# Down projections of two feed-forward layers in seven-product block form

## What is computed

```
f = (silu(h @ w_gate) * (h @ w_up)) @ w_down        # first block: x = x + gate_f * rmsnorm(f) * g
return (silu(h @ w_gate) * (h @ w_up)) @ w_down      # second block: h = h + swiglu(...), then rmsnorm_2(h)
```

## Time and profile before

| what | us |
|---|---|
| runs | 1657.09, 1657.15, 1659.39; median 1657.15 |
| span of the profiled execution | 1655.0, so about 2.15 lie outside the span |
| PE busy | 1628.8 (98%) |
| DVE busy | 1050.5 (63%) |
| ACT busy | 766.2 (46%) |
| POOL busy | 732.0 (44%) |
| first down projection, PE | 467.6 to 591.4 |
| second down projection, PE | 1520.9 to 1645.8 |

### The profile page before, as it was taken

How to read it: one execution, slowest core, us unless ns; L and a number is a source line. 1 busy time by engine, 2 the same in 40 slices (tenths; PEclk the granted TensorE clock), 3 DMA queues, 4 the chain that set the end, 5 groups by cost and what they waited for, 6 DMA issues and landing times.

```text
span 1655.0 us, 24390 instructions
## 1 busy us (share of the span) xinstructions
PE 1628.8 (98%) x9460; PEld 1399.6 (85%) x9460; DVE 1050.5 (63%) x1396; ACT 766.2 (46%) x1029; POOL 732.0 (44%) x540
## 2 busy tenths in 40 slices
PE   7999999999999999999999999999999999999997
PEld 4787899999988898888888887887888789999887
DVE  6777758999920065578778788775113699996102
ACT  4756455455543355334444546544223445544322
POOL 3342343333376635443543434445444443335663
PEclk9999999999999999999999999999999999999999
DMA  8565223333243333233332323223233323332432
GB/s 290 208 225 179 91 89 115 115 105 115 86 150 105 108 115 121 98 102 102 102 105 87 119 85 115 90 90 97 95 112 119 126 83 117 112 111 82 150 97 68
DMA packets 65127, 193.49 MB, mean 117 GB/s; under 512 B 5984, under 2 KB 8288, under 8 KB 64000
## 3 DMA queue, kind: packets, MB, share of 16 engines
q1 hardware_dynamic: 65024, 192.06, 35.3%
HBM read 183.59 MB, written 8.45 MB: 116 GB/s over the span
## 4 chain that ended last, share of the span: by engine, by line
PE 90%; DVE 7%; ACT 1%; issue 1%; DMA 1%; SPq 0%; DVEq 0%
PE PR L778 18%; PE PR L779 18%; PE PR L784 18%; PE PR L1182 4%; PE PR L1189 4%; PE PR L1184 4%; PE AX L1182 3%; PE AX L1189 3%; PE AX L1184 3%; PE PR L795 1%; PE PR L796 1%; PE PR L794 1%; PE AX L1003 1%; PE AX L1330 1%; PE AX L1334 1%
## 5 line engine op out<-in xcount | busy, mean ns | idle before, releaser
L703 POOL TENSOR_TENSOR wlo<-raw,whi 128x512 fp32r<-128x512 f32 (+1 forms) x456 | 605.8, 1354 | 631.3 <-ACT whi L1461 631.3
L1461 ACT ACTIVATE whi<-raw 128x1024 fp32r<-128x1024 f32 x216 | 225.9, 1052 | 150.0 <-PE PR L784 127.2
L778 PE MATMUL PR<-h3h,whi 128*128 128x512 f32 x608 | 245.5, 404 | 0.0
L779 PE MATMUL PR<-h3l,whi 128*128 128x512 f32 x608 | 240.4, 395 | 0.0
L722 POOL TENSOR_TENSOR wlo<-raw,whi 128x512 fp32r<-128x512 f32 x72 | 119.1, 1675 | 239.8 <-ACT whi L1719 239.8
L784 PE MATMUL PR<-h3h,wlo 128*128 128x512 f32 x608 | 154.2, 395 | 0.0
L1182 PE MATMUL PR<-ch,whi 128*128 128x256 f32 x560 | 136.0, 282 | 2.0 <-DVE gate L2509 1.2
L784 PEld LDWEIGHTS PR<-h3h,wlo 128*128 128x128 f32 x608 | 114.2, 188 | 27.6
L778 PEld LDWEIGHTS PR<-h3h,whi 128*128 128x128 f32 x608 | 114.3, 188 | 26.6 <-issue 1.2
L779 PEld LDWEIGHTS PR<-h3l,whi 128*128 128x128 f32 x608 | 114.4, 188 | 26.4 <-issue 1.0
L1184 PE MATMUL PR<-cl,whi 128*128 128x256 f32 x560 | 135.7, 281 | 0.0
(11 more groups left out here) (480 smaller groups left out, 3619.2 us busy)
## 6 DMA issues: line engine op xcount, KB each, us to landing
raw<-w SPq DMA_DIRECT2D x224, 512.0 KB, 3.4
cond<-wcond SPq DMA_DIRECT2D x48, 512.0 KB, 4.2
raw<-w SPq DMA_DIRECT2D x32, 384.0 KB, 3.2
raw<-w SPq DMA_DIRECT2D x32, 320.0 KB, 2.9
x_keep<-x SPq DMA_DIRECT2D x3, 2048.0 KB, 7.3
x<-x_keep SPq DMA_DIRECT2D x2, 2048.0 KB, 8.4
abc_a<-acum_rows SPq DMA_DIRECT2D x8, 512.0 KB, 3.9
abc_b<-acum_rows SPq DMA_DIRECT2D x8, 512.0 KB, 4.5
```

The lines of the kernel that those rows point to most:

```text
L703: ins = pool.tensor_tensor(wlo[:, j, a:a + n], raw[:, j, a:a + n], whi[:, j, a:a + n], ALU.subtract)
L778: pe.matmul(bank, whi[:, j, w], part_of(oh, k0 + k), start=first and i == 0, stop=False)
L779: pe.matmul(bank, whi[:, j, w], part_of(ol, k0 + k), start=False, stop=False)
L1461: act.activation(whi[:, j, :], raw[:, j, :], ACT.Copy).then_inc(hi_ready, 1)
```

## The change

Input tiles 4 to 19 of both down projections go into the seven-product form: input tiles in pairs (eight pairs, `PAIRS`), output tiles in pairs (four groups g, `DN_GROUPS`) and tokens in halves. The six other input tiles (`ALONE`: 0, 1, 2, 3, 20, 21) stay ordinary, as two units O1 and O2 per group. The three old row ranges and their loops are gone. Per group PE runs seven products of 24 matmuls with 256 columns and O1 and O2 with 36 matmuls of 256 columns each: 240 matmuls with 256 columns, against 132 with 512 columns. The order in a group is `DN_A`, and in the last group `DN_B`, where O1 and O2 are split by token half around S4.

What comes with it:

- Token operands: each product needs a combination of the four (input parity, token half) parts. The difference t3 and the term t1 of each pair are made by POOL inside the quads (`third`: two instructions, `third_low`: one, with 256 elements each) with one ACT instruction (`third_high`). At the start of each down projection DVE makes t2, t1l, t4a, t2l, t4b and t4l and POOL the low part of the fourth block (`last_low`), each one instruction with 2048 elements per partition, and ACT the highs b22, t1, t2 and t4, also with 2048.
- Weights: per group DVE makes four sums with 1024 elements (`dn_sum`) and the lows of units 0, 1, 3, 5 and 7 in the order of the group (`dn_low`), POOL those of units 2, 4, 6 and 8.
- Results: DVE combines the seven results (`dn_take`: p3, p4, two, g, then c12, c21, c22; in the second block also x12, x21, x22 and c11), ACT copies two of them (`take_one`, `take_c11`), squares the blocks (`dn_square`), and DVE adds the squares (`dn_acc`).
- `quad_ff_low` and `quad_ff_high` are one instruction with 512 elements per quad instead of two.
- Loads: one block A is eight weight tiles out of every second one, in runs of 512 bytes; O1 and O2 are two DMAs each.
- In the first block x is restored into `xo_a` and `xo_b` and the down result lies in `mixd`; in the second x is restored (2 MB) early in group 0, ahead of the loads of A21(1), A22(1) and O2.
- `mix_sum(3)` waits for the last accumulation of squares, which DVE makes inside `half_h(2)`, behind its second low part; two of the takes (c12, c22) stand inside `half_x(2)`.

```diff
-DOWN_K = [(0, 6), (6, 6), (12, 5), (17, 5)]
+PAIRS = 8
+ALONE = (0, 1, 2, 3, 20, 21)
+DN_A = ("A11", "S3", "A12", "S1", "S2", "S4", "O1", "A22", "O2")
+DN_B = ("A11", "S3", "A12", "S2", "A22", "S1", "S4", "O1", "O2")
...
+            def load_dn(f, g, name):
...
+                half = w22[m].rearrange("p (k two c) -> p k two c", two=2, c=P)[:, 2:10, int(name[2] == "2"), :]
+                sp.dma_start(raw[:, j, :].rearrange("p (k c) -> p k c", c=P), half).then_inc(raw_in[j], 16)
...
+            def third(s):
...
+                pool.tensor_tensor(t3[f][:, k, :], b2[:, 1, k, :], b2[:, 0, k, :], ALU.subtract).then_inc(third_ready, 1)
...
+                pool.tensor_tensor(b2[:, 0, k, :], b2[:, 0, k, :], gate_1[:, 0:T // 2], ALU.subtract).then_inc(third_ready, 1)
...
+            def last_low(f):
...
+                pool.wait_ge(*tp_at(f, "t2"))
+                pool.tensor_tensor(b2l[:, 1, :, :], b2[:, 1, :, :], b22h[:, :, :], ALU.subtract).then_inc(tl_ready, 1)
...
+            def dn_operand(f, name):
+
+                return {"A11": (b1h[:, 0, :, :], b1l[:, 0, :, :]), "A12": (b1h[:, 1, :, :], b1l[:, 1, :, :]),
+                        "S3": (t3h[f], t3l[f]), "S1": (t1h, b2l[:, 0, :, :]), "S4": (b22h, b2l[:, 1, :, :]),
+                        "S2": (t2h, t2l), "A22": (t4h, t4l)}[name]
...
-            x_sum(2)
-            mix_sum(3, V_DN1 + N_DN)
+            x_sum(2)
+            mix_sum(3, *dacc_at(0, 15), ssum_d)
...
+            def dn_first(f):
+
+                end = QUADS * f + QUADS - 1
+                token_part(f, "t2")
+                dn_ahead(f, 0, 0)
+                token_part(f, "t1l")
+                dn_sum(f, 0, "S4")
+                token_part(f, "t4a")
+                token_part(f, "t2l")
+                dn_ahead(f, 0, 1)
+                dn_ahead(f, 0, 2)
+                join(end, 6)
+                quad_ffs(end)
+                quad_ff_low(end)
+                dve.memset(ssum_d[:, :], 0.0).then_inc(dacc, 1)
+                dn_take(f, 0, "p3")
+                dn_take(f, 0, "p4")
+                token_part(f, "t4b")
+                dn_ahead(f, 0, 3)
+                dn_ahead(f, 0, 4)
+                dn_take(f, 0, "two")
+                dn_take(f, 0, "g")
+                token_part(f, "t4l")
...
+            def late_sum(k):
+
+                if k in (0, 1):
+                    dn_acc(0, DN_GROUPS - 1, "c12" if k == 0 else "c22")
```

More of the change, by code:

```diff
@@ L266, in phase_f @@
-            a("above_hth", [P, 1088])
-            ff.update({n: a(f"fq{n}", [P, 4, T], F32R) for n in (8, 9)})
-            fh_end = a("fh_end", [P, 2, T], F32R)
[L269 to L272, removed]
+                b1h = a("b1h", [P, 2, PAIRS, N], F32R, s)
+                b1l = a("b1l", [P, 2, PAIRS, N], F32R, s)
@@ new lines, in phase_f @@
+            alone.append(a("alone_b", [P, 2, 4, T], F32R))
+            fh_end = a("fh_end", [P, 2, T], F32R)
+            with ExitStack() as s:
+                up_2, turn = a("up_2", [P, T], F32, s), a("turn", [P, 8], F32, s)
+            wdt2, twice = a("wdt2", [P, 64 * KT + 64], F32R), a("twice", [P, 32])
+            return (b1h, b1l, xo_a, xo_b, hth, b2, b2l, t3, t3l, t3h, alone, t2, t4, t2l, t2h, t4l, t4h, sqx, t1h, b22h,
+                    one, two, g22, ssum_d, sq_d, wdtr, fh_end, up_2, turn, wdt2, twice)
@@ L274, in phase_first_quad @@
+        (b1h, b1l, xo_a, xo_b, hth, b2, b2l, t3, t3l, t3h, alone, t2, t4, t2l, t2h, t4l, t4h, sqx, t1h, b22h,
+         one, two, g22, ssum_d, sq_d, wdtr, fh_end, up_2, turn, wdt2, twice) = region(phase_f)
         def phase_first_quad(a):
@@ new lines, in dn_slot, with dn_loaded, dn_sum_at @@
+        def dn_slot(g, name):
+            return ({"A21": 2, "A22": 3, "A11": 0, "A12": 1, "O1": 2, "O2": 3}[name] + 2 * g) % RING
+        def dn_loaded(f, g, name):
+            upto = sum(DN_LOADS[n] for h in range(g + 1) for n in DN_BLOCKS if dn_slot(h, n) == dn_slot(g, name) and (
+                h < g or DN_BLOCKS.index(n) <= DN_BLOCKS.index(name)))
+            return raw_in[dn_slot(g, name)], 16 * (loads(U_DN[f]) // RING + upto)
+        def dn_sum_at(f, g, name):
+            return sum_ready, SUMS_FF * f + 4 * QUADS + 4 * g + ("S1", "S3", "S2", "S4").index(name) + 1
@@ L734, in _ @@
             units(U_GU1 + 4, U_ST1)
-            for s, i in POOL_LOWS:
-                quad_low(s, i)
-            units(U_DN1, U_SC)
+            blocks(0)
             for u in range(U_SC, U_SC + 4):
@@ L742, in _ @@
             units(U_SC + 4, U_ST2)
-            for s, i in POOL_LOWS:
-                quad_low(QUADS + s, i)
-            units(U_DN2, U_END - 4)
-            for u in range(U_END - 4, U_END):
-                lo(0, u)
+            blocks(1)
         @block.tensor
@@ L806, in with_low, with mix_sum @@
                 return pe.matmul(PR[:, j, c], whi[:, j, k * P:(k + 1) * P], part_of(ol, k, c), start=False, stop=k == KT - 1)
[L808 to L811 removed]
+            def mix_sum(q, ready, v, src):
+                pe.wait_ge(ready, v)
+                pe.matmul(AX[:, 0, HALF[q % 2]], con_("ones"), src[:, HALF[q % 2]], start=True, stop=True).then_inc(ss_ready, 1)
             def x_sum(q, ks=range(KT)):
```

866 lines of the change are left out of this document (646 added, 220 removed).

## The result

Beside runs of the kernel before, the changed kernel took 1682.6 us in the median (1678.5 to 1684.0, four runs) against 1657.1; ratio 1.0151, 95% interval [1.0136, 1.0167]. Run again beside other kernels it took 1680.4, ratio 1.0143 [1.0126, 1.0159]. The forecast was 1664.4, range 1654.5 to 1672: the sign was right, the loss was 25.5 us (23.4 in the second comparison) where 7.3 were forecast.

A forecast was written before the change was run, and what follows sets the result against it. PE, busy 98% of the span, was taken to bound the kernel. First down projection +2.2, its end +2.55, quads +0.5 and program end +2.0 gave +7.25 on 1657.15, so 1664.4 us; range 1654.5 to 1672.

The forecast's parts named there:

- A product in 2.84 us and a group in 28.4 without waits: Down projections: 24 matmuls take 2.84 us, a group 28.40 against 30.80 before; -19.2 us over eight groups.
- DVE and POOL in turns for the whole instruction: Start of each down projection: POOL's long low stops DVE throughout, 4.6 to 9.0 us after the start.
- the first group: Start of each down projection: 39.7 us instead of 28.4, 11.3 us of waits, twice.
- Rival C: Start of down projection: turns taken but DVE first, only S4 waits for last_low; 1654 to 1661 us; chance 0.12.
- The end of the first layer: First half done to next mixer: 16.4 us, +2.55, as mix_sum(3)'s sum comes behind two lows of half_h(2).
- that of the program: Second layer's down projection and second half: +3.2, -1.3 and +0.1 for the tail, together +2.0 us.
- the quads: POOL gets 2.4 us more per quad, DVE's idle time covers its losses; +0.5 us from the second layer's first quads.
- Rival D: Quads become bound by DVE: 0.45 us for each of 16 quads, 7 us more, 1671.6 us; chance 0.15.
- Other groups. ... No waits.: Groups after the first: DVE, POOL and ACT stay below 28.4 us, lows three units ahead; no waits.
- the restore at 1.0 us: Second layer's first group: restore of x queued ahead of three blocks, O2 among them; 1.0 us added, between 0 and 5.
- the clock: Listed with the slow rival: a fall after the 5 us wait costs some 1 to 2 us each time.

The follow-up runs named there:

- filler: Changed kernel with 72 matmuls that nobody reads put on PE ahead of S2 in the first group of both layers; median 1681.1 us.
- take_first: Changed kernel with ACT's copy take_one moved ahead of the squares in every group; median 1672.1 us, ratio 1.0088 to the kernel before.
- join_early: take_and_sum with the last quad's join, gate product and low (DVE) and high (ACT) moved ahead of S4's sum, second layer only; median 1665.3 us (1.0051).
- take_and_sum: Changed kernel with the edits of take_first and sum_before together, full result; median 1670.8 us, ratio 1.0073 to the kernel before.
- all_in: filler_end and join_early together, plus 88 filler matmuls ahead of S2 of the first group in both layers; median 1668.7 us (1.0070).
- restore_after: Changed kernel with the second layer's 2 MB restore of x issued behind O2's load of the first group; median 1684.9 us.
- sum_before: Changed kernel with the first layer's last two sums of squares added ahead of half_h(2), not inside it; median 1678.6 us.
- no_tokens: take_first with DVE's six token instructions and POOL's last_low cut to 8 elements, those products left out of the result; 1650.6 us, one execution.
- filler_end: take_and_sum with 48 matmuls that nobody reads put ahead of mix_sum(3); median 1673.5 us.

## Why the forecast was right in its cause and wrong in its size

The forecast put the span 7.25 us up; it went up 21.7. Between forecast and profile lie 1.5 + 4.2 us in the first layer's first two groups, -0.2 up to the mixer, 1.2 up to the second down projection, 4.8 + 3.4 in the second layer's first two groups and -0.4 at the end, 14.5 in all.

**Right.** A product in 2.84 us and a group in 28.4 without waits (groups 2 and 3). DVE and POOL in turns for the whole instruction: t4l was ready at D + 33.9, forecast 32.5, and the first group took 41.2, forecast 39.7. The terms within it were less good: t1l came before POOL's long instruction, not behind it, so S1 did not wait, S2's wait was 9.0 and not 5.0, and S4 did not wait, because S2 at the lower clock filled that time (in filler S4 waits 2.6 us, forecast 2.75). The sum survived because the order of turns doesn't change their total. Rival C had DVE go first; it did, for t1l, but the long instruction took the next turn and S2 paid for it, so C's saving did not come. The end of the first layer (16.2, forecast 16.4) and that of the program (16.8, forecast 17.2) were right, and the quads nearly kept their pace: 0.45 us longer in the first layer, where the forecast had nothing, and 0.4 in the second, where it had 0.5. Rival D's 7 us did not come.

**Wrong: "Other groups. ... No waits."** This is the step that failed most, 4.2 and 3.4 us, 7.6 in all. The step added up busy times and took room for granted. But DVE came out of the first group with its work late, and ACT's order puts a copy that PE needs at once behind squares that wait for DVE. Sums of busy time can't show that; the order could have, read with DVE's lateness. In the first layer the 4.2 us are 2.6 of wait and 1.6 of A12 at the lower clock. take_first took nearly all of it away (28.6 and 29.0 us).

**Wrong: the restore at 1.0 us.** It was 4.3 us (45.5 - 41.2 in the first group of the second layer), 3.2 of wait and 1.3 of clock, less 0.3 ahead of A22. The bounds in the forecast were 0 and 5, and the value taken was near the wrong one: the restore left at D + 25 and takes 8.4 us to land, with two blocks and O2 queued behind it. join_early gives 3.6 of it back.

**Undersized: the clock.** It stood as a part of rival D and not in the sum. Where it mattered it was 1.2 us at the mixer (925.6 against take_and_sum's 924.4), 1.6 of the second group's 4.2 in the first layer (A12 took 4.5 us and not 2.84) and 1.3 at O2 in the second layer. Where it stayed down longest, at S2, it cost nothing (all_in). Why it falls behind one wait and not behind another is open.

Of the 1.7 us between the mixer and the second down projection 0.4 are the quads, and the other 1.3 lie ahead of them, where the clock was low.

**A slip in the range.** It was said to begin at the middle of C, which is 1657.5; 1654.5 is near C's lower end. It changed nothing, as the result lies above the range: no rival had the second groups' loss.

**What stays open.** Of the 25.5 us between the medians (23.4 in the second comparison), 21.7 are in the profiled span. The other 2 to 4 come from executions that no profile shows; their mean granted clock was 0.984 to 0.985 against 0.987. Two places vary between profiles and are candidates, but neither was shown. Ahead of the first quads, in a part that the change doesn't touch, the profiles differ by up to 3.6 us, and in the latest of them (restore_after, D at 470.3) the granted clock was 0.95 over the first 100 us, against 0.97 in the changed kernel's. And the stretches at the lower clock vary: A12 of the second group took 4.46 us in two profiles and 2.95 in sum_before's.

**No version beats the old kernel.** no_tokens shows about what is at stake: with all the token work gone the form would win 7 us (one execution, without the sum's move and with the clock at 0.50 at the start of the mixer). With it, the layers pay 11.3 and 12.7 us for 9.6 us of matmuls each. What follows was not tried: to win, t1's, t2's and t4's lows would have to be made in small pieces where DVE and POOL have room, and the quads, with 18.64 of 20 us of DVE busy, have little.

## What to carry to other kernels

A block form that trades matmuls for sums pays in steady state and is paid for at its start, where operands are needed at once and in full: work out that first group by the order of each engine, and let a long instruction of GpSimd count against VectorE for all its time. Behind a late start, look for every short instruction that PE waits for and that stands behind one that waits for the late engine; here moving one copy up gave 6.5 us in the two down projections (8 to 10 between the medians) for nothing. Filling a wait with idle matmuls kept the clock up here, but gave nothing where another engine set the pace, and lost where the filler ran over or left a wait behind it. And compare a variant with the one that it is made from, stretch by stretch: filler_end's mixer looked 1.3 us better than the changed kernel's and was no better than take_and_sum's.

## What was not expected of the hardware

- VectorE's sum with 1024 elements showed 5.60 us because GpSimd's instruction with 2048 was ahead of it; without that, 1.22. The wait is inside the row's duration and no row names GpSimd as the releaser, so a duration far over its group's shortest is how it is found.
- A wait of 9 us brought the clock to half, and it stayed there for some 5 us of matmuls. Shorter waits gave no pattern: behind 2.5 us in the second group of the first layer a product was slowed (4.5 us), behind 3.2 us at O2 too (5.6 instead of 4.3), behind 3.2 us in the second group of the second layer none (2.9 us), all in one execution. At the mixer sum_before had 0.57 and take_and_sum 1.00 behind the same work.
- Loads of 512 KB in runs of 512 bytes landed in 4.5 us in the median (3.8 to 10.5), against 3.4 for long runs. The row is that of the changed kernel's line that loads the blocks:

```profile
DMA to landing us min/median/max: 3.8/4.5/10.5
```
